# Staging the expert weights of a mixture-of-experts layer and copying them into the ring with GpSimd

## The chip, the cores and the metric

The kernel runs on one core of one Trainium2 chip. The metric is the time of one execution in microseconds (us), as the median of several runs. Beside the timed runs there is one execution under the hardware profiler, from which all rows below come.

## What is computed

The reference is two transformer blocks in float32, for one sequence of 256 tokens, width 1024. The first block has two dense feed-forward networks and a mixer of two attentions. The second has an adaptive norm, a mixer of a convolution and an attention (mixer 2), and then a mixture of experts, which is the part that matters here:

```
logits = hf @ w_router + b_router            # 256 tokens, 32 experts, top 4 of each
for every block of tokens of one expert e:
    hc = xi @ w1[e] + b1[e]                  # w1[e]: 1024 x 2048
    g, u = hc[:, :1024], hc[:, 1024:]
    hm = (clip(u) + 1) * (g * sigmoid(1.702 * g))
    y  = hm @ w2[e] + b2[e]                  # w2[e]: 1024 x 1024
y = segment_sum(y * gate, token)
out = rms_norm(x + g2 * y)
```

## The kernel before

All weights pass through `ring`, 12 slots in SBUF of 128 partitions x 2048 float32, one MiB each. A weight piece fills one slot. In the dense stages six slots are the ring proper and the other six hold the split copies `w_hi` and `w_lo` of the pieces; there GpSimd computes `w_lo = ring - w_hi` for the pieces of mixer 2, in four instructions of 128 x 512 each (line 1594).

In the mixture of experts every expert has 12 pieces: pieces 0 to 7 are `w_exp_in` and go to slots 0 to 7, pieces 8 to 11 are `w_exp_out` and go to slots 8 to 11. SyncE (SP) issues one DMA for each piece, in the order of a loop written out by hand. Expert 0's pieces are issued during the end of mixer 2 (line 563). Then SP waits for `counts_ready`, the routing table, since the wait of every later piece depends on how many blocks of tokens the experts before it had; and then it runs a loop over experts 1 to 31 (lines 571 to 577):

```python
for j in range(SLOTS):
    sp.wait_ge(freed, before * SLOTS + (DENSE + RING + 1 - SLOTS + j))
    dst, src = expert_piece(e, j)
    sp.dma_start(dst, src).then_inc(slot_in[j], 16)
```

`before` is the number of blocks of all experts before `e`. TensorE counts `freed` up at the first matmul of each piece, so slot j is released when TensorE begins piece j + 1.

TensorE runs a loop over blocks of at most 64 tokens (up to 64 tokens of one expert). With this input there are 33 blocks for 32 experts: one expert has two. A block is, in this order: biases (line 1150); pieces 0 to 3 (function `first`, line 1119), each after a wait on `slot_in[k]`; the scatter of one half of the previous block's result (line 1130); pieces 4 to 7; the other half of the scatter; the gather of the next block's tokens (line 1103); transposes of the hidden values `gl` (line 1164), which wait for VectorE's two instructions of SBUF operands, `stt(ul, ul, 1.0, gl)` (line 1619) and `tt(gl, ul, eg)` (line 2116); the bias of the second product (line 1175); and pieces 8 to 11 (line 1184), again each after a wait on its `slot_in`. ScalarE then copies the block's result out (line 1581), which marks the end of a block in the trace. In each block VectorE also makes selection masks with `tensor_scalar` from SBUF to SBUF (lines 2061, 2103, 2065) and adds the scattered results up (line 2072). GpSimd has no work in the mixture of experts.

The large buffers lie in SBUF in the order `res`, `ring`, `nrm`, `sq`, `arena`. The tiles of the mixture of experts (`h2n`, `acc` and so on) are taken from the start of `arena`; `nrm` holds the normed input `n2_out`, which is last read by the transposes of line 1067 (semaphore `nat`).

Of the kernel before, what the change touches and what calls it, by code (L numbers as in the profile page):

```python
# [26 lines left out]
P = 128  # L27
D = 1024
KD = D // P
SEQ = 256  # L30
META = 16
TOK = SEQ + META
# [3 lines left out]
E = 32  # L36
# [10 lines left out]
PIECE = 2048  # L47
BLK = 16
RING = 6
SLOTS = 12  # L50
SPLIT_BUFS = 3
SLOT_TOK = 64
MAX_BLOCKS = E + SEQ * TOPK // SLOT_TOK
# [14 lines left out]
DENSE = MIX2_AT + MIX2_PIECES  # L68
ROUNDS = DENSE // RING
# [111 lines left out]
def build(nc, xT_in, stream, ada, c_in, cols_in, const_in, w_exp_in, w_exp_out, b_exp, out):  # L181
    ENG = mybir.EngineType
# [4 lines left out]
    PE_, ACT_, DVE_, SP_ = (ENG.PE, ENG.Activation, ENG.DVE, ENG.SP)  # L187
    ctx = ExitStack()
    with ctx:
# [3 lines left out]
        def sem(name):  # L193
            return ctx.enter_context(nc.semaphore(name))
# [5 lines left out]
        def at_place(name, shape, dt=f32, over=None):  # L200

            size = int(np.prod(shape[1:])) * 4
            offset = place[0] if over is None else over
            if over is None:
                place[0] += size
            return nc.alloc_sbuf_tensor_at(name, shape, dt, offset=offset), offset

        res, _ = at_place("res", [P, KD, TOK])
        ring, ring_at = at_place("ring", [P, SLOTS, PIECE])
        nrm, nrm_at = at_place("nrm", [P, KD, TOK])  # L210
        sq, sq_at = at_place("sq", [P, KD, TOK])
        ARENA = 16896
        arena, arena_at = at_place("arena", [P, ARENA])

        slot_bytes = PIECE * 4
        n2_out = nrm[:, :, :].rearrange("p a b -> p (a b)")[:, 0:KD * SEQ].rearrange("p (a b) -> p a b", a=KD)
        w_hi, _ = at_place("w_hi", [P, SPLIT_BUFS, PIECE], f32r, over=ring_at + RING * slot_bytes)
        w_lo, _ = at_place("w_lo", [P, SPLIT_BUFS, PIECE], f32r, over=ring_at + (RING + SPLIT_BUFS) * slot_bytes)
        x_hi, _ = at_place("x_hi", [P, KD, TOK], f32r, over=nrm_at)
        x_lo, _ = at_place("x_lo", [P, KD, TOK], f32r, over=sq_at)  # L220
        hid_hi, _ = at_place("hid_hi", [P, NF, TOK], f32r, over=arena_at)
        hid_lo, _ = at_place("hid_lo", [P, NF, TOK], f32r, over=arena_at + NF * TOK * 4)
# [6 lines left out]
        count_i = sb("count_i", [1, E + 1], i32)  # L229
# [52 lines left out]
        a = Area(arena)  # L282
# [8 lines left out]
        bias, _ = at_place("bias", [P, 3 * D], bf16, over=arena_at + BIAS_AT * 4)  # L291
# [4 lines left out]
        a = Area(arena)  # L296
# [26 lines left out]
        a = Area(arena)  # L323
# [29 lines left out]
        assert dead + 4 * SEQ <= CONST["sel"][0]  # L353


        a = Area(arena)
        h2n = a.take(2, D)
        acc = a.take(KD, SEQ)
        lgt = a.take(2, E)
# [27 lines left out]
        slot_in = [sem(f"slot_in{s}") for s in range(SLOTS)]  # L387
# [2 lines left out]
        ada_used = sem("ada_used")  # L390
        bias_in = sem("bias_in")
        bias_split = sem("bias_split")
        stored_out = sem("stored_out")
        act_chain = sem("act_chain")
        dve_chain = sem("dve_chain")
# [114 lines left out]
        @block.sync  # L510
        def _(sp):
            sp.dma_start(res[:, :, :], xT_in.rearrange("(k p) t -> p k t", p=P)).then_inc(x_in, 16)

            def load_piece(p):

                sp.wait_ge(freed, p + 1)
                sp.dma_start(ring[:, p % RING, :], stream[p, :, :]).then_inc(slot_in[p % RING], 16)

            def load_ada(n):

                if n > 1:
                    sp.wait_ge(ada_used, n - 1)
                sp.dma_start(ada_w[:, n % 2, :], ada[n, :, :]).then_inc(ada_in[n % 2], 16)

            for p in range(DENSE):
                load_piece(p)
                if p == 0:
                    sp.dma_start(col[:, :], cols_in).then_inc(cols_sem, 16)
                if p == 1:
                    sp.dma_start(c_all, c_in.partition_broadcast(P)).then_inc(c_sem, 16)  # L530
                if p == 2:
                    load_ada(0)
                    load_ada(1)
                if p == 3:
                    sp.dma_start(cst[:, NFIRST:], const_in[:, NFIRST:]).then_inc(const_rest, 16)
                if p == FFN2_AT:
                    sp.wait_ge(soft["mla"]["y"], 4)
                    sp.dma_start(c_all, c_in.partition_broadcast(P)).then_inc(c_sem, 16)
                    load_ada(ADA_FIRST)
                    load_ada(ADA_FIRST + 1)  # L540
                if p in ADA_LOADS:
                    load_ada(ADA_LOADS[p])
                if p == FFN2_AT + NF + RING:
                    sp.wait_ge(hid_split, 2 * NF + 1)
                    for i in range(3):
                        sp.dma_start(b_raw[i * E:i * E + E, :], b_exp).then_inc(bias_in, 16)

            def expert_piece(e, j):

                if j < 8:  # L550
                    return ring[:, j, :], w_exp_in[bass.ds(e * 8 + j, 1), :, :].rearrange("o p n -> p (o n)")
                return (ring[:, j, :].rearrange("p (t n) -> p t n", t=2),
                        w_exp_out[bass.ds(e * 8 + (j - 8) * 2, 2), :, :].rearrange("t p n -> p t n"))

            for j in (0, 1, 2, 3, 8, 11, 4, 5, 6, 9, 7, 10):
                if j < 5:
                    sp.wait_ge(freed, DENSE + j + 1)
                if j == 5:
                    sp.wait_ge(w_split, (POOL_ORDER[DENSE - 1] + 1) * RESTS)
                if j == 7:  # L560
                    sp.wait_ge(proj, AT[proj]["w2"] + KD)
                dst, src = expert_piece(0, j)
                sp.dma_start(dst, src).then_inc(slot_in[j], 16)
            sp.wait_ge(counts_ready, 1)
            cum = sp.alloc_register("sp_cum")
            n0 = sp.value_load(count_i[0:1, 0:1], min_val=1, max_val=4)
            sp.reg_mov(cum, 0)
            sp.reg_add(cum, cum, n0)
            with sp.Fori(1, E) as e:
                before = nc.snap(cum, engines=[SP_])  # L570
                for j in range(SLOTS):

                    sp.wait_ge(freed, before * SLOTS + (DENSE + RING + 1 - SLOTS + j))
                    dst, src = expert_piece(e, j)
                    sp.dma_start(dst, src).then_inc(slot_in[j], 16)
                n = sp.value_load(count_i[0:1, bass.ds(e, 1)], min_val=1, max_val=4)
                sp.reg_add(cum, cum, n)
            for half in range(2):
                k0, k1 = half * KD // 2, (half + 1) * KD // 2
                sp.wait_ge(fin_ready, k1)  # L580
                sp.dma_start(out.rearrange("(k p) t -> p k t", p=P)[:, k0:k1, :], fin[:, k0:k1, :])\
                    .then_inc(stored_out, 16)
            sp.wait_ge(stored_out, 32)
# [3 lines left out]
        def _(pe):  # L587
# [524 lines left out]
            def first(e, ks):  # L1112

                for k in ks:
                    pe.wait_ge(slot_in[k], e * 16 + (loaded[k] + 16))
                    for gu in range(2):
                        for j, pos, pr in halves:
                            c0 = gu * D + j * 512
                            last = mm(bank[2 + gu][pr, :], xT[:, k % 4, k // 4, :], ring[:, k, c0:c0 + 512],  # L1119
                                      start=False, stop=(k == KD - 1), tile_position=pos)  # L1120
                            if gu == 0 and j == 0:
                                last.then_inc(freed, 1)
                return last
# [20 lines left out]
            with pe.Fori(0, n_blocks) as g:  # L1144
# [33 lines left out]
                for k in range(KD):  # L1178
                    s = 8 + k // 2
                    if k % 2 == 0:  # L1180
                        pe.wait_ge(slot_in[s], e * 16 + (loaded[s] + 16))
                    for j, pos, pr in halves:
                        c0 = (k % 2) * D + j * 512
                        last = mm(bank[5][pr, :], hmT[:, k % 4, k // 4, :], ring[:, s, c0:c0 + 512],  # L1184
                                  start=False, stop=(k == KD - 1), tile_position=pos)
                        if k % 2 == 0 and j == 0:
                            last.then_inc(freed, 1)
# [400 lines left out]

        @block.gpsimd
        def _(pool):  # L1590
            for p in POOL_PIECES:
                pool.wait_ge(w_high, ORDER[p] + 1)
                for c in range(0, PIECE, REST_COLS):
                    nc.gpsimd.tensor_tensor(w_lo[:, BUF[p], c:c + REST_COLS], ring[:, p % RING, c:c + REST_COLS],  # L1594
                                            w_hi[:, BUF[p], c:c + REST_COLS].bitcast(f32),
                                            ALU.subtract).then_inc(w_split, 1)


        @block.vector
# [626 lines left out]
```

## Time and profile before

| | |
|---|---|
| median of 3 runs | 1948.34 us (1947.74 to 1951.41) |
| the profiled execution, its time | 1943.58 us |
| the profiled execution, its span from first to last instruction | 1941.8 us |
| mean granted TensorE clock | 0.98 of full |
| TensorE busy | 1832.1 us, 94% of the span |
| VectorE, ScalarE, GpSimd busy | 792.5, 506.8, 134.2 us |
| DMA | 560.9 MB, mean 289 GB/s |
| DMA in the mixture of experts | 417 to 420 GB/s in most slices |

The mixture of experts begins near 959 us and lasts to the end of the span, so it is half of the kernel. A wait in the tables below is idle time of the engine that is named first, and after the arrow stands what ended it.

### The profile page before, as it was taken

How to read it: one execution, taken by the hardware profiler on the slowest of the kernel's cores; microseconds unless marked ns; L12 is line 12 of the kernel's file. 1: busy time of each engine (PE TensorE's matmuls, PEld its weight loads, DVE VectorE, ACT ScalarE, POOL GpSimd, SP SyncE). 2: the span in 40 equal slices, each digit the busy share in tenths (PEclk: the TensorE clock that was granted, in tenths of full speed). 3: DMA queues.
4: the chain of work that ended last, by engine and by line, in shares of the span. 5: the costliest groups of instructions: out<-in, count | busy, mean ns of one | idle time of the engine just before them, and what ended most of it. 6: DMA issues, size and time to landing. Idle time of an engine off the chain costs nothing.

```text
span 1941.8 us, 28047 instructions
## 1 busy us (share of the span) xinstructions
PE 1832.1 (94%) x10776; PEld 1137.1 (59%) x10777; DVE 792.5 (41%) x1473; ACT 506.8 (26%) x830; POOL 134.2 (7%) x108
## 2 busy tenths in 40 slices
PE   7999898999899999998899999999999999999997
PEld 7999896678799989888533333233332333323333
DVE  6776532342387555756423222122222222222323
ACT  5333444532443445455211101011010110101111
POOL 0000000000000027557000000000000000000000
PEclk9999999989999999999799999999999999999999
DMA  9777442113376634324599999999999999999795
GB/s 345 266 260 264 142 174 87 65 66 139 111 277 232 219 131 152 131 109 153 216 400 418 417 419 418 418 418 417 420 417 418 419 416 419 417 417 419 310 419 202
DMA packets 98891, 560.91 MB, mean 289 GB/s; under 512 B 9008, under 2 KB 11184, under 8 KB 50480
## 3 DMA queue, kind: packets, MB, share of 16 engines
q1 hardware_dynamic: 98688, 560.02, 73.3%
q8 instruction: 41, 0.67, 0.1%
q14 instruction: 18, 0.15, 0.0%
q10 hardware_dynamic: 144, 0.07, 0.0%
HBM read 559.00 MB, written 1.05 MB: 288 GB/s over the span
## 4 chain that ended last, share of the span: by engine, by line
PE 66%; DMA 27%; ACT 3%; DVE 2%; issue 1%; POOL 0%; SPq 0%; DVEq 0%; ACTq 0%
DMA ring<-w_exp_in 26%; PE bank L601 11%; PE bank L603 11%; PE bank L602 11%; PE bank L1119 10%; PE bank L1184 5%; PE bank L705 4%; PE bank L1103 3%; PE bank L1130 2%; PE bank L595 2%; PE bank L1109 1%; ACT arena L1574 1%; PE bank L841 1%; PE bank L1175 1%; DVE arena L1619 1%
## 5 line engine op out<-in xcount | busy, mean ns | idle before, releaser
L1119 PE MATMUL bank<-ring,arena 128*64 128x512 f32 x2112 | 493.1, 601 | 44.2 <-DMA ring<-w_exp_in 41.5
L601 PE MATMUL bank<-x_hi,w_hi 128*128 128x256 f32 (+1 forms) x1272 | 371.8, 292 | 15.2 <-DVE x_lo L1675 11.2
L602 PE MATMUL bank<-x_lo,w_hi 128*128 128x256 f32 (+1 forms) x1272 | 367.1, 289 | 0.0
L603 PE MATMUL bank<-x_hi,w_lo 128*128 128x256 f32 (+1 forms) x1272 | 367.1, 289 | 0.0
L1119 PEld LDWEIGHTS bank<-ring,arena 128*64 128x64 f32 x2112 | 137.7, 136 | 363.0 <-issue 203.7
L601 PEld LDWEIGHTS bank<-x_hi,w_hi 128*128 128x128 f32 x1272 | 246.4, 194 | 26.3 <-issue 22.1
L603 PEld LDWEIGHTS bank<-x_hi,w_lo 128*128 128x128 f32 x1272 | 247.0, 194 | 0.0
L602 PEld LDWEIGHTS bank<-x_lo,w_hi 128*128 128x128 f32 x1272 | 246.3, 194 | 0.1
L1639 DVE TENSOR_TENSOR w_lo<-ring,w_hi 128x2048 fp32r<-128x2048 f32 x84 | 192.3, 2289 | 111.3 <-ACT w_hi L1242 109.2
L1184 PE MATMUL bank<-ring,arena 128*64 128x512 f32 x1056 | 232.2, 592 | 0.0
L1242 ACT ACTIVATE w_hi<-ring 128x2048 fp32r<-128x2048 f32 x110 | 210.0, 1909 | 63.4 <-PE bank L601 63.1
L1594 POOL TENSOR_TENSOR w_lo<-ring,w_hi 128x512 fp32r<-128x512 f32 x104 | 134.0, 1321 | 785.8 <-ACT w_hi L1242 785.8
L1571 ACT ACTIVATE cst<-cst 128x512 f32<-128x512 f32 x33 | 20.8, 630 | 586.2 <-DVE cst L1623 586.2
L2065 DVE TENSOR_SCALAR onehot<-cst 96x64 bf16<-96x64 f32 x66 | 16.3, 247 | 375.4 <-PE bank L1130 375.4
L1184 PEld LDWEIGHTS bank<-ring,arena 128*64 128x64 f32 x1056 | 74.1, 137 | 135.9 <-issue 133.5
L1623 DVE TENSOR_SCALAR cst<-bank 128x512 f32<-128x512 f32 x33 | 22.8, 692 | 223.0 <-PE bank L1119 223.0
L603 PE MATMUL bank<-hid_hi,w_lo 128*128 128x272 f32 (+1 forms) x352 | 100.0, 284 | 0.0
L601 PE MATMUL bank<-hid_hi,w_hi 128*128 128x272 f32 (+1 forms) x352 | 100.0, 284 | 0.0
L602 PE MATMUL bank<-hid_lo,w_hi 128*128 128x272 f32 (+1 forms) x352 | 99.7, 283 | 0.0
L2072 DVE TENSOR_TENSOR arena<-arena,bank 128x512 f32<-128x512 f32 x136 | 86.6, 676 | 8.4 <-PE bank L1130 8.4
L1130 PEld LDWEIGHTS bank<-arena 64*128 64x128 f32 x544 | 46.7, 185 | 58.5 <-issue 55.2
L1581 ACT ACTIVATE arena<-bank 128x512 f32<-128x512 f32 x33 | 19.7, 598 | 222.8 <-PE bank L1184 222.8
(291 smaller groups left out, 1892.3 us busy)
## 6 DMA issues: line engine op xcount, KB each, us to landing
ring<-w_exp_in SPq DMA_DIRECT2D x256, 1024.0 KB, 19.7
ring<-w_exp_out SPq DMA_DIRECT2D x128, 1024.0 KB, 23.1
ring<-stream SPq DMA_DIRECT2D x120, 1024.0 KB, 4.8
arena<-ada SPq DMA_DIRECT2D x48, 512.0 KB, 4.1
cst<-const_in SPq DMA_DIRECT2D x1, 1584.0 KB, 19.3
arena<-b_exp SPq DMA_DIRECT2D x3, 384.0 KB, 8.1
res<-xT_in SPq DMA_DIRECT2D x1, 1088.0 KB, 5.9
arena<-c_in SPq DMA_DIRECT2D x2, 512.0 KB, 8.4
```

The costliest lines, as they stand in the source:

```text
L601: begin = mm(out_, wh, xh, start=start, stop=False)
L602: mm(out_, wh, xl, start=False, stop=False)
L603: return begin, mm(out_, wl, xh, start=False, stop=stop)
L705: begin = last = mm(out_, w, x, start=flags[0], stop=flags[1])
L1103: last = mm(to[pr, :], S[:, t, :], h2n[:, t, 512 * j:512 * j + 512], start=(t == 0), stop=(t == 1), tile_position=pos)
L1119: last = mm(bank[2 + gu][pr, :], xT[:, k % 4, k // 4, :], ring[:, k, c0:c0 + 512], start=False, stop=(k == KD - 1), tile_position=pos)
L1130: last = mm(bank[banks[j]][:, mp * 256:mp * 256 + 256], ye[pr, mt * P:mt * P + P], ST[pr, :, :].rearrange("p a b -> p (a b)"), start=True, ...
L1184: last = mm(bank[5][pr, :], hmT[:, k % 4, k // 4, :], ring[:, s, c0:c0 + 512], start=False, stop=(k == KD - 1), tile_position=pos)
L1242: A(w_hi[:, BUF[p], :], ring[:, p % RING, :], ACT.Copy).then_inc(w_high, 1)
L1594: nc.gpsimd.tensor_tensor(w_lo[:, BUF[p], c:c + REST_COLS], ring[:, p % RING, c:c + REST_COLS], w_hi[:, BUF[p], c:c + REST_COLS].bitcast(f32),
L1639: tt(w_lo[:, BUF[p], :], ring[:, p % RING, :], w_hi[:, BUF[p], :].bitcast(f32), ALU.subtract)\
L2072: last = tt(a_, a_, bank[banks[j]][:, :].rearrange("p (a b) -> p a b", a=2), ALU.add)
```

## The change

SBUF gets six staging places of one MiB each, laid over `nrm`, `sq` and the first 7936 columns of `arena`; the tiles of the mixture of experts move 7936 columns up in `arena`. Each DMA of experts 1 to 31 now goes to staging place `j % 6` instead of slot j. GpSimd waits for the piece (`slot_in[j]`) and for the release of slot j (`freed`), copies the 128 x 2048 float32 piece into the slot with one `tensor_copy`, and counts `in_place`. TensorE waits for `in_place` in place of `slot_in`. SP waits for `in_place` of the piece six before, in place of `freed`, so it no longer needs the routing table; GpSimd now reads it and holds the running count of blocks. Expert 0 still lands in the ring directly, and GpSimd only counts its pieces. Pieces 1 to 5 of expert 1 can be issued when the same pieces of expert 0 have landed, and piece 0 when line 1067 is done.

```diff
+        stage, _ = at_place("stage", [P, STAGED, PIECE], over=nrm_at)
+        moe_at = STAGED * PIECE - 2 * KD * TOK
...
-        a = Area(arena)
+        a = Area(arena, moe_at)
...
-            sp.wait_ge(counts_ready, 1)
-            cum = sp.alloc_register("sp_cum")
-            n0 = sp.value_load(count_i[0:1, 0:1], min_val=1, max_val=4)
-            sp.reg_mov(cum, 0)
-            sp.reg_add(cum, cum, n0)
-            with sp.Fori(1, E) as e:
-                before = nc.snap(cum, engines=[SP_])
+            def stage_piece(e, j):
+
+                to, src = stage[:, j % STAGED, :], expert_piece(e, j)[1]
+                if j >= 8:
+                    to = to.rearrange("p (t n) -> p t n", t=2)
+                sp.dma_start(to, src).then_inc(slot_in[j], 16)
+
+            for j in range(1, STAGED):
+                sp.wait_ge(slot_in[j], loaded[j] + 16)
+                stage_piece(1, j)
+            sp.wait_ge(nat, 1)
+            sp.wait_ge(slot_in[0], loaded[0] + 16)
+            stage_piece(1, 0)
+            for j in range(STAGED, SLOTS):
+                sp.wait_ge(in_place, SLOTS + j - STAGED + 1)
+                stage_piece(1, j)
+            with sp.Fori(2, E) as e:
                 for j in range(SLOTS):
-
-                    sp.wait_ge(freed, before * SLOTS + (DENSE + RING + 1 - SLOTS + j))
-                    dst, src = expert_piece(e, j)
-                    sp.dma_start(dst, src).then_inc(slot_in[j], 16)
-                n = sp.value_load(count_i[0:1, bass.ds(e, 1)], min_val=1, max_val=4)
-                sp.reg_add(cum, cum, n)
+                    sp.wait_ge(in_place, e * SLOTS + (j - STAGED + 1))
+                    stage_piece(e, j)
...
-                    pe.wait_ge(slot_in[k], e * 16 + (loaded[k] + 16))
+                    pe.wait_ge(in_place, e * SLOTS + (k + 1))
...
-                        pe.wait_ge(slot_in[s], e * 16 + (loaded[s] + 16))
+                        pe.wait_ge(in_place, e * SLOTS + (s + 1))
...
+            for j in range(SLOTS):
+                pool.wait_ge(slot_in[j], loaded[j] + 16)
+                pool.sem_inc(in_place, 1)
+            pool.wait_ge(counts_ready, 1)
+            cum = pool.alloc_register("pool_cum")
+            n0 = pool.value_load(count_i[0:1, 0:1], min_val=1, max_val=4)
+            pool.reg_mov(cum, 0)
+            pool.reg_add(cum, cum, n0)
+            with pool.Fori(1, E) as e:
+                before = nc.snap(cum, engines=[ENG.Pool])
+                for j in range(SLOTS):
+                    pool.wait_ge(slot_in[j], e * 16 + (loaded[j] + 16))
+                    pool.wait_ge(freed, before * SLOTS + (DENSE + RING + 1 - SLOTS + j))
+                    pool.sem_inc(may_move, 1)
+                    nc.gpsimd.tensor_copy(ring[:, j, :], stage[:, j % STAGED, :]).then_inc(in_place, 1)
+                n = pool.value_load(count_i[0:1, bass.ds(e, 1)], min_val=1, max_val=4)
+                pool.reg_add(cum, cum, n)
```

## Rows read from the trace of the kernel before

**Rows 1.** Busy time by stage: busy us and count of each engine, clock, DMA share, GB/s
```profile
1100.00:1300.00 200.00, 188.01 (x914) 63.81 (x912) 51.55 (x113) 19.07 (x34) 0.00 (x0) 1.00 1.02 417
1500.00:1700.00 200.00, 187.48 (x910) 63.20 (x906) 51.51 (x116) 19.66 (x35) 0.00 (x0) 1.00 1.02 418
```

**Rows 2.** Timeline of ScalarE, the last instruction of blocks: start us, length us, engine, line
```profile
988.03 0.60 ACT L1581 ACTIVATE arena<-bank 128x512 f32<-128x512 f32 x1 [6.75 <-PE bank L1184]
1015.13 0.60 ACT L1581 ACTIVATE arena<-bank 128x512 f32<-128x512 f32 x1 [6.75 <-PE bank L1184]
...
1184.03 0.60 ACT L1581 ACTIVATE arena<-bank 128x512 f32<-128x512 f32 x1 [6.75 <-PE bank L1184]
1214.16 0.60 ACT L1581 ACTIVATE arena<-bank 128x512 f32<-128x512 f32 x1 [6.75 <-PE bank L1184]
...
1816.59 0.60 ACT L1581 ACTIVATE arena<-bank 128x512 f32<-128x512 f32 x1 [6.75 <-PE bank L1184]
1843.69 0.60 ACT L1581 ACTIVATE arena<-bank 128x512 f32<-128x512 f32 x1 [6.75 <-PE bank L1184]
...
1925.00 0.60 ACT L1581 ACTIVATE arena<-bank 128x512 f32<-128x512 f32 x1 [6.75 <-PE bank L1184]
```

**Rows 3.** Waits from 1300 to 1800 us: us in total, times, longest one
```profile
PEld bank L1119 <- DMA ring<-w_exp_in: 109.6, 100, 1.4
...
DVE arena L2061 <- issue: 47.4, 17, 2.8
```

**Rows 4.** Busy time by stage around the start and around the expert with two blocks
```profile
943.00:964.00 21.00, 16.62 (x77) 10.21 (x78) 10.25 (x58) 4.62 (x10) 0.00 (x0) 0.69 0.00 1
1810.00:1820.00 10.00, 10.00 (x52) 3.35 (x50) 1.47 (x7) 0.60 (x1) 0.00 (x0) 1.00 0.17 67
```

**Rows 5.** Timeline of SP and TensorE: expert 1's first issue, block 0's pieces, restart after two blocks
```profile
964.07 18.41 SPq L575 DMA_DIRECT2D ring<-w_exp_in  x8
...
959.62 8.56 PE L1119 MATMUL bank<-ring,arena 128*64 128x512 f32 x32
...
1816.37 0.60 PE L1150 MATMUL bank<-bias,onehot 96*64 96x512 bf16 x4
...
1819.75 10.10 SPq L575 DMA_DIRECT2D ring<-w_exp_in  x6
```

**Rows 6.** Timeline of GpSimd in mixer 2: with VectorE mostly elsewhere, and with VectorE on SBUF operands
```profile
815.12 4.98 POOL L1594 TENSOR_TENSOR w_lo<-ring,w_hi 128x512 fp32r<-128x512 f32 x4 [5.60 <-ACT w_hi L1242]
833.65 5.03 POOL L1594 TENSOR_TENSOR w_lo<-ring,w_hi 128x512 fp32r<-128x512 f32 x4 [4.29 <-ACT w_hi L1242]
...
897.15 16.54 POOL L1594 TENSOR_TENSOR w_lo<-ring,w_hi 128x512 fp32r<-128x512 f32 x12 [1.18 <-ACT w_hi L1242]
```

**Rows 7.** The smallest GpSimd instruction, and copies or differences of a whole piece on other engines
```profile
L2219 POOL MEMSET const-bfloat16-1.0<- 128x1 bf16 x1 | 0.1, 102 | 0.0
L1242 ACT ACTIVATE w_hi<-ring 128x2048 fp32r<-128x2048 f32 x110 | 210.0, 1909 | 63.4 <-PE bank L601 63.1
L1639 DVE TENSOR_TENSOR w_lo<-ring,w_hi 128x2048 fp32r<-128x2048 f32 x84 | 192.3, 2289 | 111.3 <-ACT w_hi L1242 109.2
```

**Rows 8.** VectorE by form before 700 us (GpSimd idle), then from 660 to 920 us (GpSimd at work)
```profile
L1675 DVE TENSOR_TENSOR x_lo<-arena,x_hi 128x256 fp32r<-128x256 f32 x8 | 3.4, 421 | 1.4 <-ACT x_hi L1248 1.1
...
L1675 DVE TENSOR_TENSOR x_lo<-arena,x_hi 128x256 fp32r<-128x256 f32 x8 | 10.9, 1371 | 0.0
```

**Rows 9.** Timeline of VectorE in one block, the two instructions that TensorE's transposes wait for
```profile
1806.27 0.69 DVE L1619 SCALAR_TENSOR_TENSOR cst<-cst 128x512 f32<-128x512 f32 x1
1806.99 0.69 DVE L2116 TENSOR_TENSOR cst<-cst 128x512 f32<-128x512 f32 x1
```

**Rows 10.** TensorE's matmuls of the pieces, whole kernel: count, busy us, mean ns
```profile
L1119 PE MATMUL bank<-ring,arena 128*64 128x512 f32 x2112 | 493.1, 601 | 44.2 <-DMA ring<-w_exp_in 41.5
```

More of the change, by code:

```diff
@@ L50 @@
 SLOTS = 12
+STAGED = 6
 SPLIT_BUFS = 3
@@ L392, in build @@
         bias_split = sem("bias_split")
+        in_place = sem("expert_piece_in_place")
+        may_move = sem("expert_piece_may_move")
         stored_out = sem("stored_out")
@@ L563, in _ @@
                 sp.dma_start(dst, src).then_inc(slot_in[j], 16)
-            sp.wait_ge(counts_ready, 1)
-            cum = sp.alloc_register("sp_cum")
-            n0 = sp.value_load(count_i[0:1, 0:1], min_val=1, max_val=4)
-            sp.reg_mov(cum, 0)
-            sp.reg_add(cum, cum, n0)
-            with sp.Fori(1, E) as e:
-                before = nc.snap(cum, engines=[SP_])
-                for j in range(SLOTS):
-                    sp.wait_ge(freed, before * SLOTS + (DENSE + RING + 1 - SLOTS + j))
-                    dst, src = expert_piece(e, j)
-                    sp.dma_start(dst, src).then_inc(slot_in[j], 16)
-                n = sp.value_load(count_i[0:1, bass.ds(e, 1)], min_val=1, max_val=4)
-                sp.reg_add(cum, cum, n)
+            loaded = [16 * ROUNDS if s < RING else 0 for s in range(SLOTS)]
+            def stage_piece(e, j):
[13 more added lines that the diff above has]
+            with sp.Fori(2, E) as e:
+                for j in range(SLOTS):
+                    sp.wait_ge(in_place, e * SLOTS + (j - STAGED + 1))
+                    stage_piece(e, j)
             for half in range(2):
@@ L1590, in _ @@
         def _(pool):
+            loaded = [16 * ROUNDS if s < RING else 0 for s in range(SLOTS)]
             for p in POOL_PIECES:
```

## The prediction

> **What bounds the kernel now.** I read the busy time by stage first, then the timeline of the block ends, then the waits. Up to 959 us the change touches almost nothing: only SP's queue after expert 0, and GpSimd's after its last split piece. So only the mixture of experts counts. There DMA moves 418 GB/s with all its engines busy, in stretch after stretch, while GpSimd does nothing [rows 1]. A piece is 1.0486 MB, which at 418 GB/s is 2.51 us, and twelve are 30.1 us. The block ends show the same: in the steady part a block ends every 1214.16 - 1184.03 = 30.13 us, but near the start and after the expert with two blocks one ends every 27.10 us [rows 2]. So 27.1 us is what TensorE's block costs when its weights are there, 30.1 us is what the transfers allow, and the 3.0 us between them are TensorE's waits for pieces 0 to 7 [rows 3]. The steady part is bound by DMA, with TensorE 3 us behind it.
>
> DMA loses time in two places [rows 4]: from 943 to 964 us it moves nothing, because all 12 slots are full and SP first waits for the routing table and then for slot 0; and from 1810 to 1820 us its share is 0.17, because the expert with two blocks holds its slots for a second block. The second stretch ends with an issue at 1819.75, 3.4 us after the second block's first instruction at 1816.37 [rows 5].
>
> **The change, part by part.**
>
> *Earlier transfers (a gain).* Five pieces of expert 1 now follow expert 0's without a pause, and the sixth follows when line 1067 is done; at 943 us DMA has nothing else to do. The sixth has landed by about 943 + 6 x 2.51 = 958 us. Slot 0 is released after block 0's first piece: four pieces take 8.56 us from 959.62 on [rows 5], so about 962.0. Before, the first issue was at 964.07. So DMA restarts at about the old time but six pieces ahead, and 6 x 2.51 = 15.1 us of transfer is saved if transfers stay the bound. SP's own waits cost nothing, as long as a copied piece comes back sooner than the five others in staging take to land (12.5 us).
>
> *The copy (the cost that decides).* GpSimd gets 31 x 12 = 372 copies of 128 x 2048 float32, 12 for each expert, in series. Only a copy of 2.5 us or less fits in the time of a transfer. No row shows such a copy. The nearest is GpSimd's own difference of a whole piece, four instructions in 4.98 to 5.03 us, 1.25 us each [rows 6]. Its smallest instruction takes 0.10 us [rows 7], which I take as the fixed part: (1.25 - 0.10) / 512 = 2.246 ns for an element. That instruction reads two operands and writes one; the copy reads one and writes one.
> - Above: as slow as the difference, 2048 x 2.246 ns + 0.10 = 4.70 us.
> - Below: if only the two reads set the time, half of it, 2.40 us. A still lower end comes from the other engines' instructions on a whole piece, 1.91 us on ScalarE and 2.29 us on VectorE [rows 7].
> - Between: if each of the three operands costs a third, the copy costs two thirds, 2048 x 1.497 ns + 0.10 = 3.17 us. I take this one, since the row of the same engine is nearer than those of others, and since nothing in it says that its write is free.
>
> The Trainium skill says two things here, in "GPSIMD Engine Reference". Section 4.1 calls one-input work on GpSimd "roughly line-rate"; at the page's 1.2 GHz a copy would by estimate be 2048 / 1.2 = 1.71 us and a little, and the change would gain. Section 3.1 gives a best case of about 1.8 cycles for an element, by estimate 3.07 us, and the change would lose. No run here shows a one-input GpSimd instruction of any size, so the page leaves the question open.
>
> *The port between VectorE and GpSimd.* When VectorE worked on SBUF operands beside it, GpSimd's twelve instructions took 16.54 us instead of 12 x 1.25 = 15.0 [rows 6]: 0.13 us for each. A block has ten such VectorE instructions (2 + 4 of lines 2061 and 2103, 2 of line 2065, and the two of rows 9), so 1.3 us for an expert, or 0.11 for a copy. In the other direction VectorE pays far more: 1371 ns instead of 421 for the same instruction [rows 8]. TensorE's block may become up to a copy longer for each of the two instructions that it waits for [rows 9]. At a copy of 3.2 us the block has some 12 us to spare, which hides it.
>
> *Waits and queues.* TensorE waits for `in_place` in the order of the pieces, which is also the order in which it uses them. GpSimd's register work and its load of a count between experts I cost at nothing, because its queue can go on under a copy of 3 us. If it can't: VectorE idles 2.8 us ahead of its masks, where it loads four such values [rows 3], so one load is 0.7 us, 31 of them 22 us, and these go into the range. The shift of the tiles in `arena` costs nothing.
>
> **The sum.** One copy with its share of the port is C = 3.17 + 0.11 = 3.28 us, an expert 39.4 us against 30.1. GpSimd is then the bound from 962.0 on. 372 x 3.28 = 1220.2. To this comes one stop at the expert with two blocks: GpSimd can't copy the next expert's first piece until TensorE has used the last piece (a piece is 32 / 4 = 8 matmuls, 1.8 us in the 27.1 us block) and begun the second block (3.4 us [rows 5]), 5.2 us together. After the last copy TensorE has 1.8 us of that piece, and from the last block's end at 1925.00 [rows 2] to the end of the span are 16.8 us. Span: 962.0 + 1220.2 + 5.2 + 1.8 + 16.8 = 2206.0. The early transfers gain nothing, since the copies start at 962 whatever has landed. The profiled execution's own time was 1.8 us above its span, and the median of the runs 4.8 us above that: 2206.0 + 1.8 + 4.8 = 2212.6. I predict **2212 us**, 13.5% slower.
>
> For any C two paths compete: GpSimd's, 985.8 + 372 C, and TensorE's, which after expert 28's last piece has four blocks of 27.1 us to run: 962.0 + 336 C + 1.8 + 108.4 + 16.8 = 1089.0 + 336 C. The second equals the span before at C = 2.54. That is the point from which the sign turns, and 0.01 us of C is 3.4 to 3.7 us of span.
>
> **Rivals.**
>
> *The copy keeps pace (faster).* If a copy costs 1.8 to 2.4 us, DMA stays the bound. For it speak the other engines' rows [rows 7] and the reads-only bound; against it, that it needs GpSimd's write to be free. The gain is 15.1 us, less the copy that each piece now passes through before use (2.1), less some 2 us by which VectorE's two instructions are late in the blocks bound by TensorE: 11 us, span 1931 (the second formula at 2.51 gives 1932), median 1938.
>
> *GpSimd as slow as with two inputs (much slower).* C = 4.81, span 985.8 + 372 x 4.81 = 2775, median 2782. For it speaks that the row's time could be the loop and not the operands.
>
> *VectorE's lock with a fast copy (slower).* With a fast copy GpSimd is still at work about 80% of the time, and each of the two instructions of [rows 9] may wait for a whole copy: 27.1 + 2 x 1.9 = 30.9 us against 30.1, 0.8 us in each of some 28 blocks, 22 us. Against the gain of 15.1 - 2.1 = 13 us that makes 9 us slower than before, median 1958. It decides once the two waits together pass 3.0 us. Against it: the first of them meets a copy at a chance point, so about 2.8 us is likelier. The Trainium skill ("SBUF — State Buffer", Who interferes with whom) says that the later of the two engines "fully blocks"; the 1371 ns agree with it.
>
> *In between.* C from 2.51 to 2.8: by the second formula a span from 1932 to 2030, median near 1990.
>
> **Chances.** Two thirds or near it (C 2.8 to 3.5): 0.52. Keeps pace: 0.30. As slow as two inputs (C above 3.5): 0.08. In between: 0.07, of which 0.02 within 0.2%. The lock: 0.03. Faster or slower is by over 0.2%, 3.9 us, about the spread of the three runs. So faster 0.30, same 0.03 (0.02 of it from in between, 0.01 from the lock), slower 0.67. The range has to hold the keeps-pace case and the likeliest: from 1930 to 2285 (C = 3.48 by the first formula, or 3.28 with the 22 us of loads and another 50 us); out of it are the 0.08 and a few hundredths above and below. The likeliest case's own range is 2090 (C = 2.95) to 2285.
>
> **What the changed profile would show.** Right: GpSimd busy nearly all of the time from 962 us on, one copy behind the other, 372 of about 3.2 us; block ends every 39 us; DMA at about 320 GB/s with its share near 0.77; TensorE waiting for GpSimd's line and no longer for DMA; no DMA gap at 943 us, but one just before 962. The VectorE instructions of [rows 9] at up to 3 us. Wrong: copies under 2.5 us with gaps between them, and block ends every 30.1 us with DMA at 418; then the sum fails at the two-thirds step. TensorE's granted clock was 0.69 on average in the idle-ridden stretch from 943 to 964 us [rows 4]. If it fell to its 1.2 GHz level in the longer waits too, the matmuls of 601 ns [rows 10] would double, and the time would come out above the range.

## The result and the profile after

| | before | changed |
|---|---|---|
| median | 1948.09 us (4 runs) | 1937.85 us (4 runs, 1935.55 to 1938.75) |
| ratio | | 0.9945, 95% interval 0.9932 to 0.9958 |
| span of the profiled execution | 1941.8 us | 1936.7 us |

The change made the kernel 0.55% faster. The prediction was 2212 us; its first rival, "the copy keeps pace", had said 1938 us. The step that decides is on the page's list of costliest groups of the changed kernel:

```profile
L1627 POOL COPY ring<-stage 128x2048 f32<-128x2048 f32 x372 | 717.0, 1933 | 256.2 <-DMA stage<-w_exp_in 104.3
L1132 PE MATMUL bank<-ring,arena 128*64 128x512 f32 x2112 | 479.4, 598 | 19.9 <-POOL ring L1627 19.8
```

A copy takes 1.93 us in the mean (median 1.896), not 3.17. Ahead of the copies GpSimd's idle time ends mostly with a landing (104.3 us on `w_exp_in` and 60.3 on `w_exp_out`, of 256.2), so GpSimd waits for DMA and not the other way. The busy time by stage and the block ends answer to [rows 1, 2]:

```profile
1100.00:1300.00 200.00, 192.71 (x976) 70.57 (x974) 102.55 (x125) 20.25 (x36) 154.40 (x81) 1.00 1.02 418
1500.00:1700.00 200.00, 182.95 (x910) 65.00 (x912) 99.14 (x115) 18.84 (x34) 154.25 (x80) 1.00 1.02 418
```

```profile
992.75 0.60 ACT L1594 ACTIVATE arena<-bank 128x512 f32<-128x512 f32 x1 [6.75 <-PE bank L1197]
1020.32 0.60 ACT L1594 ACTIVATE arena<-bank 128x512 f32<-128x512 f32 x1 [6.75 <-PE bank L1197]
...
1268.90 0.60 ACT L1594 ACTIVATE arena<-bank 128x512 f32<-128x512 f32 x1 [6.75 <-PE bank L1197]
1299.00 0.60 ACT L1594 ACTIVATE arena<-bank 128x512 f32<-128x512 f32 x1 [6.75 <-PE bank L1197]
...
1811.07 0.60 ACT L1594 ACTIVATE arena<-bank 128x512 f32<-128x512 f32 x1 [6.75 <-PE bank L1197]
1838.17 0.60 ACT L1594 ACTIVATE arena<-bank 128x512 f32<-128x512 f32 x1 [6.75 <-PE bank L1197]
...
1919.96 0.60 ACT L1594 ACTIVATE arena<-bank 128x512 f32<-128x512 f32 x1 [6.75 <-PE bank L1197]
```

The steady part is as before, 418 GB/s and 30.1 us from block to block. What changed is how long TensorE runs free of DMA at the start: the first eleven blocks, up to 1268.90, come 27.6 us apart. In the kernel before the sixth block (27.35 us after the fifth, which ended at 1096.43) was already a little late, and the seventh came 30.15 us after it:

```profile
1123.78 0.60 ACT L1581 ACTIVATE arena<-bank 128x512 f32<-128x512 f32 x1 [6.75 <-PE bank L1184]
1153.93 0.60 ACT L1581 ACTIVATE arena<-bank 128x512 f32<-128x512 f32 x1 [6.75 <-PE bank L1184]
```

From the first block's end to the end of the expert with two blocks' first block it is 1811.07 - 992.75 = 818.3 us, against 1816.59 - 988.03 = 828.6 before: 10.2 us won. The four blocks after it and the tail give 0.4 back. The two spans differ by 5.1 us only, because in this one profile the first block ended 4.7 us later, and so did the stages ahead of it, which the change doesn't touch (ScalarE reached the same instruction of block 0 at 961.09 and at 956.38 us). In the comparisons below I therefore use, beside the medians, **the expert part of a profile**: from block 0's end to the end of the span. It was 953.8 us before and 944.0 us changed.

Where the 10 us come from is to be seen in the changed kernel's busy time by stage, last columns (DMA share, GB/s), against [rows 4]:

```profile
943.00:958.00 15.00, 12.65 (x71) 12.28 (x72) 7.20 (x39) 4.02 (x9) 0.00 (x0) 0.61 1.02 420
958.00:970.00 12.00, 9.99 (x36) 3.07 (x34) 4.75 (x22) 0.60 (x1) 1.22 (x1) 0.75 0.34 141
970.00:985.00 15.00, 14.94 (x77) 5.61 (x74) 10.21 (x16) 1.65 (x3) 11.76 (x7) 1.00 0.83 323
```

DMA now works from 943 to 958 us and a few us longer, where it moved nothing before. As all of this comes 4.7 us later in this profile, the first of it is still expert 0, and the six pieces, 15.1 us, end near 962. DMA then stops, as forecast, and restarts when the first copy (968.8 to 970.7 us) has freed a place.

The pause near 1811 us [rows 4] is filled too: from 1810 to 1820 us DMA's share is 0.99 (397 GB/s) where it was 0.17. That gains nothing. The four blocks behind it take 108.9 us, 108.4 before, since TensorE bounds them in both kernels; DMA is only done earlier.

### The profile page after: what moved, and what is told of

Its sections match the earlier page's. It is cut to its first block, busy times and chain, and to the rows that moved or that the text cites. A ratio compares the mean times of both kernels' runs of the same rounds, so it can differ in the third digit from the quotient of the medians.

```text
span 1936.7 us, 29530 instructions
## 1 busy us (share of the span) xinstructions
PE 1815.9 (94%) x10776; PEld 1145.6 (59%) x10777; DVE 1024.0 (53%) x1473; ACT 506.7 (26%) x830; POOL 851.2 (44%) x481
## 4 chain that ended last, share of the span: by engine, by line
PE 62%; DMA 25%; DVE 4%; POOL 4%; ACT 3%; issue 2%; SPq 0%; POOLq 0%; DVEq 0%; ACTq 0%
DMA stage<-w_exp_in 24%; PE bank L614 11%; PE bank L616 11%; PE bank L615 11%; PE bank L1132 10%; PE bank L1197 5%; POOL ring L1627 4%; PE bank L718 4%; PE bank L608 2%; PE bank L854 1%; PE bank L1143 1%; DVE cst L1652 1%; DVE arena L1652 1%; PE bank L1008 0%; PE bank L1010 0%
## 5 line engine op out<-in xcount | busy, mean ns | idle before, releaser
L1627 POOL COPY ring<-stage 128x2048 f32<-128x2048 f32 x372 | 717.0, 1933 | 256.2 <-DMA stage<-w_exp_in 104.3
L1132 PE MATMUL bank<-ring,arena 128*64 128x512 f32 x2112 | 479.4, 598 | 19.9 <-POOL ring L1627 19.8
L1197 PE MATMUL bank<-ring,arena 128*64 128x512 f32 x1056 | 232.2, 592 | 0.0
L2098 DVE TENSOR_SCALAR onehot<-cst 96x64 bf16<-96x64 f32 x66 | 103.5, 1567 | 237.4 <-PE bank L1143 237.4
L2136 DVE TENSOR_SCALAR arena<-cst,small 128x64 f32 x132 | 100.8, 824 | 0.0
## 6 DMA issues: line engine op xcount, KB each, us to landing
stage<-w_exp_in SPq DMA_DIRECT2D x248, 1024.0 KB, 12.6
```

Source lines behind the costliest of these rows:

```text
L1627: nc.gpsimd.tensor_copy(ring[:, j, :], stage[:, j % STAGED, :]).then_inc(in_place, 1)
L2098: return V.tensor_scalar(to[0:3 * E, :], const("ones", 0, SLOT_TOK, 3 * E), cst[0:3 * E, bass.ds(e_ + CONST["eye3"][0], 1)], None, ALU.mult)
L2136: V.tensor_scalar(SG[:, t, i, :], slots(b), place, weight, ALU.is_equal, ALU.mult)
```

## The experiments

Two theories of the gain were to be told apart. The lead theory: the gain is the six pieces fetched in the pause at 943 us. The two-block theory: it is the pause of [rows 4] near 1811 us, about as long, which six more places can bridge too. The first run does that, and direct landing further down does it again.

**Start late.** SP begins with expert 1 only when slot 0 is released, as before.

```diff
+            sp.wait_ge(counts_ready, 1)
+            sp.wait_ge(freed, DENSE + RING + 1)
             for j in range(1, STAGED):
```

> SP starts with expert 1's pieces only when slot 0 is released, as in the kernel before; all else as changed. Lead theory (the whole gain is the six pieces fetched between 943 and 964 us, 15.1 us, of which the copy takes back 1.9 at the restart and 1.9 on each piece's way, and VectorE's wait for the port 1.5): the gain is gone and two of the costs stay, 1.9 + 1.5, so about 3.4 us slower than the kernel before, some 1951.5 us. Two-block theory (the gain is the pause of DMA near 1811 to 1820 us, filled by the six places): still some 8 us faster than the kernel before.

Measured: 1955.91 us, ratio to before 1.0039 (1.0024 to 1.0055). The gain is gone, which refutes the two-block theory; the loss was 8.5 us against a forecast of 3.4. SP issues pieces 1 to 5 ahead of piece 0, and GpSimd copies piece 0 first. The timeline of SP and GpSimd in this run:

```profile
967.34 22.94 SPq L576 DMA_DIRECT2D stage<-w_exp_in  x8
...
986.19 14.75 POOL L1629 COPY ring<-stage 128x2048 f32<-128x2048 f32 x8 [62.56 <-DMA stage<-w_exp_in]
```

The first copy starts 18.9 us after the first issue. So I repeated it with piece 0 first:

```diff
-            for j in range(1, STAGED):
-                sp.wait_ge(slot_in[j], loaded[j] + 16)
-                stage_piece(1, j)
+            sp.wait_ge(counts_ready, 1)
+            sp.wait_ge(freed, DENSE + RING + 1)
             sp.wait_ge(nat, 1)
-            sp.wait_ge(slot_in[0], loaded[0] + 16)
-            stage_piece(1, 0)
+            for j in range(STAGED):
+                sp.wait_ge(slot_in[j], loaded[j] + 16)
+                stage_piece(1, j)
```

> As late_start, but expert 1's piece 0 is issued first, not sixth. Theory: late_start lost 4 us more than the 3.4 forecast because GpSimd could copy nothing before piece 0 had landed as the last of six; with it first, the time from block 0's end to the end of the span is 953.8 + 3.4 = 957.2 us, some 3.4 us slower than the kernel before, 1951 us. Rival: the order is harmless and the copies themselves cost 8 us; then it stays at 962 us, 1956 us.

Measured: 1949.2 us, ratio 1.0007 (0.9995 to 1.0018); the expert part 954.4 us, against 962.4 in late_start. So the order had cost most of the loss. Staging all pieces without the early start gains nothing that shows. What it costs is known only roughly: 1.3 us by the medians, with an interval from -1.0 to 3.5, so the 3.4 us forecast is not excluded; 1.9 us by the profiles, 0.6 in the expert part and 1.3 in block 0, which the expert part leaves out. A likely reason that it is less than forecast is that the six places also fill the short gaps that DMA had after its restart (shares of 0.92 and 0.86 between 964 and 990 us before). In 972 to 1000 us the share is now 1.00:

```profile
966.00:972.00 6.00, 6.00 (x24) 1.94 (x22) 2.52 (x13) 0.00 (x0) 0.00 (x0) 0.73 0.11 16
972.00:1000.00 28.00, 26.45 (x138) 9.86 (x136) 16.05 (x23) 2.81 (x5) 18.46 (x10) 1.00 1.00 413
```

**Three places in place of six** (`STAGED = 3`, the tiles in `arena` left where they are).

> Three staging places in place of six. Lead theory: three pieces are fetched early, 7.5 us, less 3.8 for the copy and 1.5 for the port, a gain of 2.2 us, some 1946 us; block ends in the steady part stay 30.1 us apart. Two-block theory: three places fill 7.5 of the 10 us, so some 1940 us. Third possibility: three places are too few to keep DMA busy while a copy runs; then blocks come more than 30.1 us apart and the time is above the kernel before.

Measured: 2104.13 us, ratio 1.0785 (1.075 to 1.082). The third possibility came true. From the page, DMA issues (KB each, median us from issue to landing):

```profile
stage<-w_exp_in SPq DMA_DIRECT2D x248, 1024.0 KB, 7.0
stage<-w_exp_out SPq DMA_DIRECT2D x124, 1024.0 KB, 7.1
```

A place is taken for 7.0 us of transfer and 1.9 us of copy; with three places that is 8.9 / 3 = 2.97 us for a piece, 35.6 us for an expert, and blocks came 32 to 40 us apart, 36.6 in the mean of the steady part. With six places the transfers queue behind each other (12.6 us to landing) and DMA is never short of work.

**Direct landing from expert 12 on.** If only the head start counts, the copies are needed while the lead is used up, and no longer. From expert 12 on SP again waits for `freed` and lands in the ring, and GpSimd only counts.

```diff
+            with sp.Fori(DIRECT_FROM, E) as e:
+                before = nc.snap(cum, engines=[SP_])
+                for j in range(SLOTS):
+                    sp.wait_ge(freed, before * SLOTS + (DENSE + RING + 1 - SLOTS + j))
+                    dst, src = expert_piece(e, j)
+                    sp.dma_start(dst, src).then_inc(slot_in[j], 16)
...
+            pool.wait_ge(in_place, DIRECT_FROM * SLOTS)
+            with pool.Fori(DIRECT_FROM, E) as e:
+                for j in range(SLOTS):
+                    pool.wait_ge(slot_in[j], e * 16 + (loaded[j] + 16))
+                    pool.sem_inc(in_place, 1)
```

> Experts 1 to 11 are staged and copied; from expert 12 on, where blocks already come 30.1 us apart, the pieces land in the ring as in the kernel before, and GpSimd only counts them. Lead theory: the six pieces of lead are kept as transfer already done, and the copy on the way (1.9 us) and the port (1.5 us) are saved: about 3.4 us faster than the changed kernel, 1934.5 us. Two-block theory: the places are needed at expert 28, and the time goes back to that of the kernel before, about 1948 us.

Measured: 1938.21 us, ratio 0.9954 (0.9935 to 0.9972), not to be told from the changed kernel by its median; but the expert part of its profile was 939.6 us. So both were timed again, on one chip:

> The changed kernel once more, on the same chip as the next run. Lead theory: 0.9945 of the kernel before, about 10 us faster, and from block 0's end to the end of the span 944 us as in its first profile.

> Copies for experts 1 to 11 and direct landing from expert 12 on, timed beside the changed kernel. Lead theory: from block 0's end to the end of the span 939.6 us as in its first profile, against 944 for the changed kernel and 953.8 before; so about 4 us under the changed kernel in the median, 1934 us where the kernel before takes 1948. Rival: the first profile was a lucky one in the blocks too, and both kernels take the same.

Measured: the changed kernel 1938.18 us, ratio 0.9946 (0.9927 to 0.9966), expert part 943.9; direct landing 1934.27 us, ratio 0.9935 (0.9917 to 0.9953), expert part 1931.5 - 991.16 = 940.3. The expert part is 4.4 and 3.6 us shorter in the two pairs of profiles, and the medians of the second pair differ by 3.9. The intervals of the two ratios overlap, so that it beats the kernel before is shown, and that it beats the changed one rests on the profiles. The gain stays although expert 28, the one with two blocks, lands directly, which speaks against the two-block theory once more. At the switch the timeline of switch12_again has one block of 27.1 us, where a piece no longer waits for its copy:

```profile
1297.28 0.60 ACT L1612 ACTIVATE arena<-bank 128x512 f32<-128x512 f32 x1 [6.75 <-PE bank L1215]
1324.39 0.60 ACT L1612 ACTIVATE arena<-bank 128x512 f32<-128x512 f32 x1 [6.75 <-PE bank L1215]
1354.18 0.60 ACT L1612 ACTIVATE arena<-bank 128x512 f32<-128x512 f32 x1 [6.75 <-PE bank L1215]
```

**What a GpSimd instruction costs.** Three kernels, each run once, put another operation in the copy's place, `tensor_tensor` with the same output: the staged piece added to itself, the slot's old content subtracted from it, and added to it. They leave out the plain copy, so experts 1 to 31 compute with other weights; they serve for the times alone.

```diff
-                    nc.gpsimd.tensor_copy(ring[:, j, :], stage[:, j % STAGED, :]).then_inc(in_place, 1)
+                    nc.gpsimd.tensor_tensor(ring[:, j, :], stage[:, j % STAGED, :], stage[:, j % STAGED, :],
+                                            ALU.add).then_inc(in_place, 1)
```

> The copy is an addition of the staged piece to itself, so that experts 1 to 31 get doubled weights: two operands read in place of one, same size. If the second operand is what makes GpSimd's difference of 128 x 512 take 1.25 us, a piece takes 0.10 + 2048 x 2.246 ns = 4.70 us, and by 985.8 + 372 x (4.70 + 0.11) the span is about 2775 us, blocks 57.7 us apart. If it is not, and the copy of a whole piece is quick for another reason, its size for one, a piece takes about 1.9 to 2.5 us and the span stays near 1937 us.

> The copy is the staged piece minus what the slot held, so experts 1 to 31 get other weights: two different operand tiles and a subtraction, as in mixer 2's differences. If the operation or the two tiles make mixer 2's instruction slower than two reads, a piece takes 0.19 + 2048 x 2.08 ns = 4.45 us, as the difference of 128 x 512 in 1.25 us has it, blocks 54 us apart, a span near 2660 us. If only the reads count, it takes 3.60 us as the addition did, span 2360 us; then mixer 2's 1.25 us come from its size or its float32r output.

> The staged piece plus what the slot held (so experts 1 to 31 get sums of weights): two different operand tiles as in subtract_tiles, the addition as in two_inputs. If the operation makes the difference between 3.60 and 4.52 us a piece, it takes 3.60 us, blocks 43.7 us apart, span near 2360 us. If the two different tiles make it, it takes 4.5 us, blocks 54.6 us apart, span near 2705 us.

Measured, from the view of one line: the copy of the changed kernel, the addition of a tile to itself, the subtraction and the addition of two tiles (duration in ns, least, median, most).

```profile
L1627 POOL COPY ring<-stage x372: 1892/1896/2440, 968.8 to 1896.2; 128x2048 f32<-128x2048 f32 x186
```

```profile
L1627 POOL TENSOR_TENSOR ring<-stage x372: 3592/3597/4072, 970.0 to 2333.8; 128x2048 f32<-128x2048 f32 x186
```

```profile
L1627 POOL TENSOR_TENSOR ring<-stage,ring x372: 4484/4521/4995, 970.3 to 2677.1; 128x2048 f32<-128x2048 f32 x186
```

```profile
L1627 POOL TENSOR_TENSOR ring<-stage,ring x372: 4488/4515/4986, 969.3 to 2675.6; 128x2048 f32<-128x2048 f32 x186
```

The second operand adds 1.70 us if it is the same tile and 2.62 us if it is another; addition and subtraction make no difference (4.52 and 4.52). If each operand read costs the same r and the write nothing, 1.896 = f + 2048 r and 3.597 = f + 2 x 2048 r give r = 0.83 ns for an element and a fixed part of f = 0.19 us. Copies alone bear this out: four short copies for a piece (below) take 0.612 us each at 512 columns, so from 512 to 2048 columns a copy grows by (1.896 - 0.612) / 1536 = 0.84 ns for an element. A copy's read and write together thus cost no more than the second read alone, and nothing is left for the write. A second, different tile costs 1.28 ns. In subtract_tiles and add_tiles that tile is also the output; in mixer 2's difference the output is a third tile, and its 1.25 us still fit: 0.19 + 512 x (0.83 + 1.28) ns = 1.27. So writing over an operand isn't the cause. The spans were 2359.8, 2705.3 and 2704.1 us.

**Near the break-even point.** 768 columns by the addition to itself, 1280 by a copy; here too the weights are other ones, and the kernel ran once.

> Of each piece 768 columns are the staged values added to themselves (so these weights are doubled) and 1280 are copied. By the two kinds' measured times, 0.19 us fixed and 0.83 ns for each operand read of an element, a piece takes 0.19 + 1.28 + 0.19 + 1.07 = 2.73 us, 0.2 us above a transfer. Break-even theory (point at 2.54): the span is about 1089.0 + 336 x (2.73 + 0.11) = 2043 us, blocks 34 us apart. If the staging places level it out, the span stays near that of the kernel before.

Measured: 2009.3 us (before 1947.94), span 2007.4, blocks 32.33 us apart in the steady part, which is 2.69 us for a piece. The two groups of GpSimd from the view by form:

```profile
L1627 POOL TENSOR_TENSOR ring<-stage 128x768 f32<-128x768 f32 x372 | 557.8, 1499 | 51.1 <-PE bank L1132 50.7 <-PE bank L1197 0.5
L1629 POOL COPY ring<-stage 128x1280 f32<-128x1280 f32 x372 | 478.3, 1286 | 0.0
```

With 2.69 the prediction's second formula gives 1993 us, and 6 more because the copies started at 968.1 and not 962.0: 1999 against 2007. Half of the rest is the last four blocks, which took 112.7 us and not 108.4. The places level nothing out: 0.18 us of a piece above a transfer cost 60 us.

**Four short copies for a piece.**

```diff
-                    nc.gpsimd.tensor_copy(ring[:, j, :], stage[:, j % STAGED, :]).then_inc(in_place, 1)
+                    for c in range(0, PIECE, 512):
+                        last = nc.gpsimd.tensor_copy(ring[:, j, c:c + 512], stage[:, j % STAGED, c:c + 512])
+                    last.then_inc(in_place, 1)
```

> Each copy as four of 128 x 512. If the fixed part of a GpSimd instruction is 0.10 us, a piece takes 1.85 + 0.3 = 2.15 us. Port theory: VectorE's instruction of 2.23 us in the steady part falls to about 1.1, since it waits for a quarter only, and blocks bound by TensorE go from 27.63 to about 27.2 us; in all 0.3 to 1 us faster than the changed kernel, about 1937 us. Rival: GpSimd's instructions follow each other without a gap for VectorE, then VectorE stays at 2.2 us and the time is 0.6 us above the changed kernel.

Measured: 2148.48 us, ratio 1.1028 (1.1003 to 1.1052), against both forecasts. GpSimd isn't the bound: from 1300 to 1800 us it is busy for 367 of 500 us. The timeline of VectorE and GpSimd in one block, first GpSimd, then VectorE:

```profile
1394.58 26.30 POOL L1628 COPY ring<-stage 128x512 f32<-128x512 f32 x47
...
1396.17 0.78 DVE L2096 TENSOR_SCALAR arena<-cst,small 128x64 f32 x2 [2.78 <-issue]
1396.87 2.32 DVE L2138 TENSOR_SCALAR arena<-cst,small 128x64 f32 x4
1408.41 12.53 DVE L2100 TENSOR_SCALAR onehot<-cst 96x64 bf16<-96x64 f32 x1 [9.22 <-PE bank L1143]
1420.85 1.27 DVE L2107 TENSOR_TENSOR arena<-arena,bank 128x512 f32<-128x512 f32 x2
```

47 copies run in a row to 1420.88, and VectorE's mask of line 2100, 0.25 us when GpSimd is idle, takes 12.53 us and ends when they end. The sums behind it (line 2107) are late, and TensorE, which waits for them, is idle 7 us in each block. Its matmuls are also slower, at a mean granted clock of 0.88 from 1300 to 1800 us (1.00 in the changed kernel): it is busy about 29.6 us in a block, where 27.1 were enough. Blocks come 36.4 us apart. I tried one reason, that an instruction without a semaphore update lets nobody in:

```diff
+                        last.then_inc(in_place if c == PIECE - 512 else may_move, 1)
```

> Each piece as four copies of 128 x 512, now each with a semaphore update of its own. In the first run of quarters VectorE waited 12.5 us for the port beside 23 copies in a row, while in mixer 2 it got a turn beside each of GpSimd's 128 x 512 differences, which all had an update. If the update is what lets VectorE in, its mask of line 2100 falls from 5.6 us to under 1 us and blocks come 30.1 us apart again. If it is the short one-input copy that leaves no gap, blocks stay 36 us apart and the span near 2150 us.

Measured: 2152.39 us, blocks again 36 us apart, and the mask again at 12.53 us. The reason falls. Why the masks of lines 2096 and 2138 get a turn beside the same copies (0.4 and 0.6 us each) and the one of line 2100 doesn't is open. Copies of a whole piece don't do it: there each mask waits for one copy at most. Nor is it the unbroken row alone: in two_inputs 329 additions of a whole piece ran without a gap, and no mask took more than 3.64 us, one addition.

## Why the prediction was wrong

- **The bound before.** Right: 30.1 us by DMA, seen again in the changed kernel, late_start, late_start_0_first and the two runs of switch12; 27.1 by TensorE, seen again in the last blocks, and 27.6 where copies run beside it.
- **The copy, "two thirds of the difference".** This is the step that failed, at 3.17 us for what takes 1.90, below the 2.51 us of a transfer and not above. It spread 2.246 ns evenly over two reads and a write. The operation runs show that the write costs nothing beside the reads, that the second read of the row was dearer than the first (1.28 ns against 0.83) because it came from another tile, and that the fixed part is 0.19 and not 0.10 us. Even the bound "only the reads count", 2.40 us, was too high, since it halved a row whose two reads aren't alike. Only the other engines' 1.91 and 2.29 us were near [rows 7]; that ScalarE's is within 0.02 us is chance as far as the runs show. The Trainium skill's two sentences in "GPSIMD Engine Reference" split the same way: Section 4.1's "roughly line-rate" holds for this copy (0.83 ns for an element is one cycle at the page's 1.2 GHz), and Section 3.1's best case of 1.8 cycles, which it gives for an unrolled loop, doesn't. The same section of the Trainium skill also gives 1.03 cycles for a loop body that is bound by its read and write ports; the prediction didn't weigh that figure, and the copy is near it.
- **The sum and the sign's turning point.** The formulas hold with the measured C. In the runs in which GpSimd was the bound, C was 3.64 (two_inputs) and 4.55 (subtract_tiles) from the distance of the blocks; the first formula gives 2340 and 2678 against spans of 2359.8 and 2705.3. Of the 20 and 27 us that are missing 8 are the later start of the copies. The rest is in the sum's stops and its end. It had one stop of 5.2 us; the traces have two, 8.7 and 9.0 us in expert 1, whose eighth copy waits for block 0 to free its slot, which the sum left out, and 6.4 and 10.1 us at the expert with two blocks. The last block ended 5.2 and 6.5 us after the last copy, and not 1.8. The point of 2.54 us lies between the changed kernel and part_two_inputs, as it should.
- **Earlier transfers.** Right in size and place: 15.1 us, and with them taken away (late_start_0_first) the ratio is 1.0007. In the text they were a gain only for the first rival, since with slow copies they are worth nothing; that was right too.
- **The first rival's working.** 1938 against 1937.85, and that close by luck: its span, 1931, was for a gain of 11 us, and 10.2 were measured. The copy on the way costs 1.9 (said: 2.1). VectorE costs 1.5 (said: 2): that is what TensorE's wait for it, 2.40 us in place of 0.86, puts once between a piece's landing and the block's end. The rival left out that the copy is paid a second time, since DMA restarts only when the first place has been copied out. The two smaller costs and DMA's short gaps after the restart, a little better filled, made up for about half of that. DMA's idle time after 943 us is what settles it: before 21.0 in the pause and 3.2 after; changed 8.0 (958 to 970 at 0.34 of 1.02) and 2.8 (970 to 985 at 0.83), so 13.4 us less, to a few tenths; less 1.9 and 1.5 is 10.0, and 10.2 were measured.
- **The port.** GpSimd's share was said to be 0.11 us for a copy; 1.933 against 1.896 makes 0.04. For VectorE the forecast was up to a copy for each of the two instructions of [rows 9]. Only the first waits (median 2.23 us of 33, the second 0.69 in all 33), on the timeline of the changed kernel:

```profile
1467.93 1.90 POOL L1627 COPY ring<-stage 128x2048 f32<-128x2048 f32 x1 [0.66 <-DMA stage<-w_exp_out]
1468.14 2.23 DVE L1652 SCALAR_TENSOR_TENSOR cst<-cst 128x512 f32<-128x512 f32 x1
...
1470.40 0.69 DVE L2149 TENSOR_TENSOR cst<-cst 128x512 f32<-128x512 f32 x1
1470.49 2.36 POOL L1627 COPY ring<-stage 128x2048 f32<-128x2048 f32 x1 [0.66 <-DMA stage<-w_exp_out]
```

  A copy comes every 2.5 us, so after the first wait VectorE is through both (2.23 + 0.69 us) as the next copy begins, and that copy pays (2.36). TensorE waits 2.40 us instead of 0.86, and its 3 us of slack in the steady part keep that from adding up block by block. So the lock rival's point, two waits of over 3.0 us, isn't reached.
- **Waits and queues.** Right to cost GpSimd's register work and loads at nothing: in two_inputs and in subtract_tiles it ran 329 instructions in a row, over 27 experts, without a gap. The 22 us for them in the range weren't needed.
- **The chances.** 0.30 stood on what happened, but the range's low end was all that covered it. The weight lay on the nearest row of the same engine; that row was one of two operands, and how its time splits could not be read from it.

## What to carry to other kernels

A price for an operation that the trace doesn't have should not be made by dividing a row of another operation; where the sign turns on it, as here at 2.54 us, the row only says that the question is open. More landing places for a stream bound by DMA are worth what DMA can fetch while it would otherwise stand still, here six pieces in one pause of 21 us, and nothing after that. The second pause was filled too and brought nothing, because the blocks behind it were bound by TensorE. So the copies that make the places usable can stop as soon as the lead is spent. Before a copy is cut into short ones, look who waits for the other engine at its port.

## What the runs showed of the hardware

- GpSimd on 128 x 2048 float32 in SBUF: a copy 1.896 us, a tile added to itself 3.597, two different tiles added or subtracted 4.515 and 4.521.
- A row of 47 GpSimd copies of 128 x 512, 0.61 us each and one every 0.56 us, held up one VectorE instruction with operands in SBUF for 12.53 us, until the row ended, while others got in after one copy. Beside GpSimd's copies and additions of 128 x 2048 no mask waited longer than for one of them.
- Transfers of one MiB reach 418 GB/s with six in turn, and about 340 with three, each landing 7.0 us after its issue.
- TensorE's granted clock was 1.00, its 2.4 GHz level, from 980 to 1920 us of the changed kernel, with waits up to 2.4 us in each block; in quarters, with one of 7 us in each block, it was 0.88 from 1300 to 1800 us, and in the addition and subtraction of two tiles, with blocks 54.6 us apart, its mean over the run fell to 0.87.
